# Start addresses of eight weight buffers and two operand regions moved by 16 to 96 bytes in a two-layer transformer kernel

## The reference

```python
def _conv_ffn(h, w_in, conv_w, conv_b, w_out):
    t = h.shape[1]
    u = h @ w_in                                   # 2048 -> 2 x 5632
    up = jnp.pad(u, ((0, 0), (CONV_WIDTH - 1, 0), (0, 0)))
    c = conv_b + up[:, 0:t] * conv_w[0]
    for j in range(1, CONV_WIDTH):
        c = c + up[:, j:j + t] * conv_w[j]
    gate, val = jnp.split(c, 2, axis=-1)
    return (jax.nn.silu(gate) * val) @ w_out       # 5632 -> 2048

def reference(...):
    h = x
    for i in range(DEPTH):                         # DEPTH = 2
        a = _rmsnorm(h, norm_mix[i])
        y = _mla(a, ...) if i == 0 else _swa_sinks(a, ...)
        h = h + y
        h = h + _conv_ffn(_rmsnorm(h, norm_ffn[i]), ...)
    return _rmsnorm(h, final_norm)
```

## The kernel before

| tensor | before | after the change |
|---|---|---|
| `raw0..3` | 0, 0, 0, 0 | 0, 0, 0, 0 |
| `w_hi0..3`, and `w_lo0..3` alike | 0, 0, 0, 0 | 0, 96, 16, 112 |
| `h`, `half_b`, `cg`, `cv`, `up` | 0 | 0 |
| `op_in` and all else in `ra` | 32 | 32 |
| `op_ffn`, `op_att`, `op_lat` and all else in `rg` | 32 | 96 |

## Time and profile before

### The profile page before, as it was taken

How to read it: one execution, slowest core, us unless ns; L and a number is a source line. 1 busy time by engine, 2 the same in 40 slices (tenths; PEclk the granted TensorE clock), 3 DMA queues, 4 the chain that set the end, 5 groups by cost and what they waited for, 6 DMA issues and landing times.

```text
span 2038.8 us, 33732 instructions
## 1 busy us (share of the span) xinstructions
PE 1987.1 (97%) x11624; PEld 1750.3 (86%) x11624; DVE 1442.4 (71%) x1990; ACT 1018.4 (50%) x1233; POOL 171.9 (8%) x237
## 2 busy tenths in 40 slices
PE   8899999999999999999999789999999999999998
PEld 7698888888888888888898568888888888888887
DVE  7766777887787786555566768877887887755554
ACT  6456455555545554443344864555455555533433
POOL 1102230000000000110020313200000000001110
PEclk9999999999999999999999899999999999999998
DMA  7467555555555555556576225555555555555553
GB/s 279 134 198 172 176 186 188 196 183 195 194 176 186 195 195 191 191 179 196 194 250 200 79 65 185 185 195 193 178 185 195 195 177 202 188 192 189 188 192 107
DMA packets 103874, 374.36 MB, mean 184 GB/s; under 512 B 11547, under 2 KB 12124, under 8 KB 103548
## 3 DMA queue, kind: packets, MB, share of 16 engines
q1 hardware_dynamic: 101180, 362.55, 53.3%
q0 software_dynamic: 2624, 10.83, 2.1%
HBM read 364.94 MB, written 8.39 MB: 183 GB/s over the span
## 4 chain that ended last, share of the span: by engine, by line
PE 91%; DVE 3%; issue 1%; ACT 0%; DVEq 0%; ACTq 0%
PE ps L397 57%; PE ps L400 30%; DVE scores_sb L1212 1%; DVE probs L1241 1%; PE ps L428 1%; PE ps L427 1%; PE ps L426 1%; PE ps L562 0%; PE ps L609 0%; PE ps L600 0%; PE ps L602 0%; DVE w_lo L1017 0%; ACT w_hi L746 0%; PE ps L687 0%; PE ps L611 0%
## 5 line engine op out<-in xcount | busy, mean ns | idle before, releaser
L1017 DVE TENSOR_TENSOR w_lo<-raw,w_hi 128x1024 fp32r<-128x1024 f32 (+1 forms) x682 | 828.6, 1229 | 516.5 <-ACT w_hi L746 493.7
L397 PE MATMUL ps<-op_in,w_hi 128*128 128x512 f32 x3248 | 1116.8, 392 | 9.5 <-DVE w_lo L1017 9.5
L746 ACT ACTIVATE w_hi<-raw 128x1024 fp32r<-128x1024 f32 (+1 forms) x682 | 715.2, 1055 | 817.1 <-PE ps L400 657.4
L400 PE MATMUL ps<-op_in,w_lo 128*128 128x256 f32 x3248 | 882.9, 282 | 0.0
L397 PEld LDWEIGHTS ps<-op_in,w_hi 128*128 128x128 f32 x3248 | 597.2, 188 | 122.8 <-issue 8.4
L400 PEld LDWEIGHTS ps<-op_in,w_lo 128*128 128x128 f32 x3248 | 614.6, 189 | 17.0
L397 PE MATMUL ps<-op_ffn,w_hi 128*128 128x512 f32 x1408 | 486.2, 390 | 0.0
L400 PE MATMUL ps<-op_ffn,w_lo 128*128 128x256 f32 x1408 | 391.7, 282 | 0.0
L397 PEld LDWEIGHTS ps<-op_ffn,w_hi 128*128 128x128 f32 x1408 | 262.2, 188 | 53.0
L400 PEld LDWEIGHTS ps<-op_ffn,w_lo 128*128 128x128 f32 x1408 | 266.1, 189 | 2.7
L397 PE MATMUL ps<-op_att,w_hi 128*128 128x512 f32 x512 | 176.3, 392 | 2.5 <-issue 2.5
(11 more groups left out here) (185 smaller groups left out, 1210.7 us busy)
## 6 DMA issues: line engine op xcount, KB each, us to landing
raw<-weights SPq DMA_DIRECT2D x666, 512.0 KB, 3.6
raw<-weights SPq DMA_DIRECT2D x16, 384.0 KB, 3.1
bias_rows<-brow POOLq DMA_DIRECT2D x1, 6144.0 KB, 36.2
win_bias<-bias_rows POOLq DMA_DIRECT2D x4, 1024.0 KB, 8.8
h<-xt SPq DMA_DIRECT2D x8, 256.0 KB, 7.8
x_tok<-x_rows SPq DMA_DIRECT2D x2, 1024.0 KB, 10.5
y<-yt SPq DMA_DIRECT2D x4, 512.0 KB, 4.0
par<-params SPq DMA_DIRECT2D x1, 352.0 KB, 11.5
```

The costliest lines, as they stand in the source:

```text
L397: return mm(ps[:, bank, 0:2 * T], whi, op, start=start, stop=stop)
L400: return mm(ps[:, bank, 0:T], wlo, op[:, 0, :], start=False, stop=False)
L746: f(w_hi[s][:, 0:cols], raw[s][:, 0:cols], ACT.Copy).then_inc(hi_ready, 1)
L1017: v.tensor_tensor(w_lo[s][:, 0:cols], raw[s][:, 0:cols], w_hi[s][:, 0:cols].bitcast(F32), ALU.subtract).then_inc(lo_ready, 1)
```

## The change

It moves start addresses and nothing else. Each `w_hi` and `w_lo` buffer gets 16 more elements (64 bytes), and begins 0, 32, 16 or 48 bytes into its room, for slots 0 to 3. Before `ra` the allocation is set to 32 bytes past a multiple of 128, and before `rg` 64 more bytes are skipped. The list of instructions on every engine, their shapes, waits and order are the same before and after.

```diff
     raw = [new(f"raw{s}", [P, CH]) for s in range(SLOTS)]
-    w_hi = [new(f"w_hi{s}", [P, CH], F32R) for s in range(SLOTS)]
-    w_lo = [new(f"w_lo{s}", [P, CH], F32R) for s in range(SLOTS)]
+    SHIFT = (0, 8, 4, 12)
+
+    def shifted(name, s):
+        return new(f"{name}{s}", [P, CH + 16], F32R)[:, SHIFT[s]:SHIFT[s] + CH]
+    w_hi = [shifted("w_hi", s) for s in range(SLOTS)]
+    w_lo = [shifted("w_lo", s) for s in range(SLOTS)]
     h = new("h", [P, KT, T])
...
+    top[0] = top[0] // 128 * 128 + 160
     ra = region(KT * 2 * T * 4)
     op_in = place("op_in", [P, KT, 2, T], F32R, ra)
...
+    region(64)
     rg = region(FT * 2 * T * 4)
     r_o = rg + 57344
     op_ffn = place("op_ffn", [P, FT, 2, T], F32R, rg)
```

## The result

The changed kernel takes 2053.19 us in the median (2051.81 to 2054.22, 4 runs), the kernel before in the same comparison 2038.09 us. The ratio is 1.007, with a 95% interval of 1.0057 to 1.0082: slower, clear of the 0.2% that can be told. The forecast was 2038.4 us, no change.

What follows compares the result with a forecast made beforehand. TensorE's matmul pairs were taken to bound the kernel. Every term of the change was taken at 0 (attention 0 to 1 us), leaving the profiled 2040.6 us, less 2.2 us for a median: 2038.4 us, range 2025 to 2055.

Steps and rivals of the forecast that it cites:

- What bounds the kernel: TensorE's matmul pairs set the time: 1847 us, 91% of the span of 2038.8 us.
- 5328 pairs: On TensorE, a high matmul of 512 columns and a low one of 256 each; 0.3467 us a pair.
- the pair's non-scaling part: In each TensorE pair, 26.7 ns that do not scale with the clock, 142 us over all pairs.
- Instructions, writers, clashes between engines: No instruction added, ScalarE and VectorE writes to shifted buffers no slower, no interference with TensorE's reads: 0 us each.
- TensorE's two reads: Loaded weights and streamed activations in a matmul: their new start addresses were taken to cost 0 us.
- one experiment of its own: Eight `token_chunk` matmuls with load at 32 and stream at 0 bytes, roles exchanged: 0.119 us each against 0.12.
- Rival A: TensorE's pace does not depend on start addresses at all; the forecast itself, 2038.4 us, chance 0.57.
- Rival B: TensorE weight loads begun off a multiple of 64 bytes take one piece more: 14 us slower, 2052 us, chance 0.22.
- B's own signs: Chunks of slots 1 to 3 longer than slot 0's, by the low-to-high step alone, 118 to 122 ns.
- Rival C: TensorE's two reads clash at distance 32 modulo 64; new distances free some slots: 13 us faster, 2025 us, chance 0.21.
- The objection raised against it: A TensorE load reads at half the stream's pace, so their distance runs through all values whatever the starts.
- The range: Whole kernel, to hold 8 in 10: 2025 to 2055 us, about 0.07 above and 0.1 below.

Runs made afterwards that it cites:

- e3: Kernel before with all weight halves and both operand regions begun 32 bytes further; 2040.04 us, ratio 1.0003.
- e2: Kernel before with only the operand regions moved, to 32 and 96 bytes past multiples of 128; 2052.17 us, ratio 1.0061.
- e4: Kernel before with all weight halves begun 32 bytes further, operand regions as before; 2069.2 us, ratio 1.0151.
- e11: Kernel before with all weights 8 bytes past a multiple of 128, distance 88 for op_in, 120 for op_ffn and op_att; 2058.13 us.
- e10: Kernel before with all weights 8 bytes past a multiple of 128, distance 24 for op_in, 56 for op_ffn and op_att; 2058.33 us.
- e8: Kernel before with all weights 24 bytes past a multiple of 128, distance 40 for op_in, 8 for op_ffn and op_att; 2062.53 us.
- e12: Kernel before with all weights 24 bytes past a multiple of 128, distance 72 for op_in, 104 for op_ffn and op_att; 2046.68 us.
- e15: Kernel before with all low weight halves begun 32 bytes past a multiple of 128, high halves and operands as before; 2029.1 us, ratio 0.995.
- e16: Kernel before with low weight halves at 16 bytes, high halves at 0, op_ffn and op_att at 96 past a multiple of 128; 2050.71 us.
- e17: Kernel before with low weight halves at 48 bytes, high halves at 0, op_ffn and op_att at 96 past a multiple of 128; 2046.15 us.
- e6: Kernel before with all weights 16 bytes past a multiple of 128, distance 16 for op_in, 48 for op_ffn and op_att; 2064.64 us.
- e7: Kernel before with all weights 16 bytes past a multiple of 128, distance 80 for op_in, 112 for op_ffn and op_att; 2051.9 us.
- e13: Kernel before with high weight halves 32 bytes past a multiple of 128, low at 0, op_ffn 32 further; 2067.57 us, ratio 1.0137.

## Why the prediction was wrong, point by point

**What bounds the kernel.** Right. The loss is 5328 pairs at some 3 ns each, as the sensitivity worked out there says (1 ns a pair is 5.3 us), and the pair's non-scaling part was the right room to look in.

**Instructions, writers, clashes between engines.** Right, each at 0. L1023 and L752 keep 1231 and 1059 ns. In e3 the weights and operands move against `raw`, `h` and everything else, and the counts differ by one matmul at most.

**TensorE's two reads, taken at 0.** This is the step that failed. It called the exchange of roles in `token_chunk` "one experiment of its own" and took its result, 0.119 against 0.12 us, as the nearest row. What the runs showed in its place is 2.6 ns more a pair on `op_in` and 3.4 on `op_ffn`, 15 us. The step also said that its row covers the move of the `rg` tensors from 32 to 96; e2 makes that very move, and the pair on `op_ffn` goes from 346.3 to 352.7 ns. The row could not show the effect. `token_chunk` has matmuls of 256 columns alone, and in e4 and in the changed kernel it is the step behind the 512 columns that grows. Its distance, streamed start minus loaded start, is 0 - 32, which is 96 modulo 128: a place where pairs lose 6 ns, and the row looked clean. e4 has `token_chunk` at 0. Its timeline at 113.5 us:

```profile
113.50 0.28 PE L428 MATMUL ps<-w_hi,op_lat 128*128 128x256 f32 x1
...
114.45 0.28 PE L430 MATMUL ps<-w_hi,op_lat 128*128 128x256 f32 x1
```

Eight matmuls in 0.95 us, as before, in the kernel that loses 5.7 to 6.4 ns in every pair. By the start times of all such steps in layer 0, a matmul of `token_chunk` takes 118.2 ns in the kernel before (96), 119.3 in e4 (0) and 117.7 in e2 (32). So the stretch is blind to the exchange that was asked of it, 32 against 96, where pairs differ by 6 ns. It isn't blind to every placement: where its streamed operand begins 8 bytes off a multiple of 16 it takes 120.7 to 123.4 (e11, e10, e8, e12). The step also knew that it did not cover 16, 112 and most distances, and still took 0 for all of it.

**Rival A, the pace doesn't depend on the starts, 0.57.** Wrong: 343.9 to 352.9 ns over the runs.

**Rival B, a ninth piece for loads off a multiple of 64, 14 us, 2052 us, 0.22.** The number is within 1.2 us of the result, and it is a coincidence. e3 has all loads 32 past a multiple of 64 and loses nothing; e15 has half of them so and gains; the low halves at 16 and 48 on `op_in` (e16, e17) take 346.8 and 346.7 ns, as at 0. B's own signs were that the chunks of slots 1 to 3 are longer than those of slot 0, and by the step from low to high alone. That step did not grow (118.3 and 118.4 ns, above), and with all weights at 16 it is 121.3, 116.1, 117.5 and 118.2 ns at distances 16, 48, 80 and 112 (e6, e7), which is no fixed ninth piece. As means over the stage, slots 0 to 3 take 2788, 2809, 2818, 2788 ns a chunk in `f0_out` of the changed kernel (2774 to 2775 each before) and 2788, 2775, 2820, 2814 in `f0_in`, its first chunk left out (before 2773, 2776, 2786, 2778). A turn of the four slots on `op_ffn` as most of them are, with the first high matmuls of slots 0, 1, 2, 3, 0:

```profile
874.53 0.39 PE L403 MATMUL ps<-op_ffn,w_hi 128*128 128x512 f32 x1
...
877.31 0.40 PE L403 MATMUL ps<-op_ffn,w_hi 128*128 128x512 f32 x1
...
880.12 0.40 PE L403 MATMUL ps<-op_ffn,w_hi 128*128 128x512 f32 x1
...
882.94 0.39 PE L403 MATMUL ps<-op_ffn,w_hi 128*128 128x512 f32 x1
...
885.73 0.39 PE L403 MATMUL ps<-op_ffn,w_hi 128*128 128x512 f32 x1
```

2.78, 2.81, 2.82 and 2.79 us. Slot 0, whose weights start where they always did, grew on both operands, and slot 1, whose weights moved, did not grow on `op_in`. Neither fits a cost of shifted loads.

**Rival C, the two reads get in each other's way by their distance, 0.21.** This one came nearest: the two reads do act on each other by their distance, and the sign was the other, for I let the old distance be the bad one. The objection raised against it, that a load reads at half the pace of the stream and so runs through all distances anyway, is refuted by e3 and e4. The curve foretells the change's size roughly, a third to a half too high: the mean of distances 96, 0, 80, 112 is 350.8 ns, and `op_ffn` measured 349.7; of 32, 64 (2.83 us a chunk), 16, 48 it is 350.7, and `op_in` measured 349.4. It does not foretell the slots: slot 0 at distance 96 takes 2788 ns a chunk in the changed kernel and 2826 in e2, where all slots are at 96. Nor did any pair come near the 325 ns that C quotes from the Trainium skill, "TensorE: Matmul & The Clock Gate" (Back-to-back issue gap); the shortest is 343.9.

**The range.** 2025 to 2055 held the 2053.2, but by the price of B, whose mechanism is out; that is luck. Chances of 0.57 for no change rested on the blind row; with it set aside, the kernel stood at one known distance and was being moved to seven unknown ones, and nothing in the profile said that the known one was average.

The prediction quoted the Trainium skill, "SBUF — State Buffer" (Who interferes with whom), that TensorE never waits on another engine; the counts of e3, equal to one matmul though its weights lie elsewhere against all that VectorE and ScalarE write, agree. The same page gives TensorE two independent read ports, one for each operand. The runs do not show the ports, but they show that the two reads are not independent in time, and there the measurement decides. As for its lines of 16 bytes (Specifications), weights that begin 8 bytes off such a line are not slow as such: their pairs take 347.0 to 351.2 ns (e8, e10, e11, e12), those of whole lines 346.8 to 352.9.

**What stays open.** That the start addresses set the pace is shown, and by e3 and e4, for a move of 32 bytes, that it is the distance between the two operands and not the start of either; how they do it is not. The distance modulo 128 gives the pace on one operand to 0.3 ns where all slots are alike and one pace is held ((32, 32) at three placements, (32, 0) at two), but not where slots differ, and (32, 64), (96, 80) and (96, 48) have two paces each. The pace jumps between neighbours ((32, 0) 344.8, (32, 16) 346.8, (32, 32) 346.8, (32, 96) 352.5), and both loads take part. Why a pair at one place can run at either of two paces, and what picks one, is open. Half of the stretch at 1.2 GHz is 320 ns, so 24 ns of every pair remain at the best place. Of all pairs of distances fewer than 30 were tried.

## What to carry to other kernels

In a kernel like this one, where TensorE is the bound and loads a new weight block for every matmul, a buffer's start address is a tuning parameter: with instructions, waits and the other engines' work untouched, the distance between the loaded and the streamed operand moved this kernel from 2029 to 2069 us. Fix it on purpose, by trying a few multiples of 32 bytes for each operand, since an allocation made earlier shifts it unseen; and read it as matmuls counted in a long window, where 0.1% shows. A few matmuls of a timeline can mislead, since the pace may change within a stage. And before a row is taken as witness that an effect is absent, ask whether that row would show it if it were there.

## What the runs showed of the hardware that was not expected

- With the clock granted in full and no idle time, a high and a low matmul took 343.9 to 352.9 ns a pair, by start addresses alone.
- Where all slots are alike the period is 128 bytes, to 0.3 ns: moving `op_in` by 128 left 346.8 ns at 347.1, moving `op_ffn` by 192 made 346.3 into 352.7.
- It is steady, not scatter: in e13 each chunk of `f1_out` takes what its twin in `f0_out` took, to 2 ns. But one placement can have two paces: (32, 64) runs at 346.7 ns a pair for 21 chunks and at 353.3 for the rest.
- The cost of the change and of e4 is in the step from the high matmul (512 columns) to the low one: 228.8 ns before, 231.6 and 235.9 after; the step behind the 256 columns kept 118.3, 118.4 and 117.0. It isn't so everywhere: at distance 16 (e6) both steps are longer, 231.7 and 121.3.
- Matmuls of 256 columns alone do not answer to 32 against 96: 117.7 and 118.2 ns each, where pairs differ by 6 ns. With the streamed operand 8 bytes off a multiple of 16 they take up to 123.4.
- Parts of a placement do not add: 2056.1 us with the weights' shifts alone, 2052.2 with the operands' alone, 2053.2 with both.
